# Hybrid attention layer in fp32 on TensorE: the rotary part of the softmax scores as two products of stacked rows instead of three

## The chip, the cores and the metric

The kernel runs on one core of one Trainium2 chip, in one launch. The metric is the device time of a run in microseconds (us); less is better. All data is fp32. Large matrix products are done in a "high and low" form: an operand x is split into xH, its value rounded to the matmul type fp32r, and xL = x - xH, again in fp32r. A product of two such operands is the sum of three matmuls (high times high, high times low, low times high) into one PSUM bank.

## The reference, cut to what matters

One decoder layer: an input projection that feeds two groups of heads (stick-breaking attention, 8 heads of 64; softmax attention with low-rank queries and keys, 4 heads), an output projection with a residual, and a SwiGLU feed-forward part. There are 1024 tokens and 1024 model columns. What matters here is the softmax group. Each of its heads has 128 plain columns (NOPE) and 64 rotary columns (ROPE); the rotary key is one for all four heads:

```python
def causal_softmax_attention(q, k, v):        # q, k: 192 columns a head, v: 128
    scale = MLA_QK_DIM ** -0.5
    for i in range(S // BLOCK_Q):
        s = einsum('bthd,bshd->bhts', q[:, q0:kend], k[:, :kend]) * scale
        p = softmax(where(causal, s, -inf), axis=-1)
        outs.append(einsum('bhts,bshd->bthd', p, v[:, :kend]))
...
q = concatenate([q[..., :128], apply_rope(q[..., 128:], positions)], axis=-1)
k_rope = broadcast_to(apply_rope(k_rope, positions), (B, S, 4, 64))
k = concatenate([k_nope, k_rope], axis=-1)
```

## The kernel before, in words

**Stages.** The program goes through input projections, an up-projection of queries and keys by token tiles of 128 (`up_tile`), the softmax heads, the stick-breaking heads, the output projection and the feed-forward part. The engines run one instruction list each and meet at semaphores. Tokens are held in reverse order, so the keys that a query tile may see are the columns from its own start to the end of the row.

**Softmax heads.** The four heads are worked in two pairs p, two heads e in each. A unit is one query tile of one head. `UNITS` lists 16 units for a pair: both heads go through the tiles in `ORDER0 = [7, 1, 5, 3, 2, 4, 0, 6]`, and tile i has 8 - i blocks of 128 keys, so a head's units have 1, 7, 3, 5, 6, 4, 8 and 2 blocks. This text numbers the units 0 to 31 through both pairs (unit 0 has 1 block, unit 1 has 7, unit 8 has 1 again) and writes S(u) for the scores, T(u) for the transposes and V(u) for the products with the values of unit u.

- S(u) on TensorE (`qk`, `mla_scores`, L1901 to L1907, through `three`, L1688): for each chunk of up to 512 keys, three matmuls of the plain columns (`mqH`, `mqL` with `mkH`, `mkL`), three of the rotary columns, all with 128 contraction rows, and in the first chunk one small bf16 matmul that adds the causal mask. There are 12 chunks in a head and 48 in all.
- `nmx` on VectorE (L1374) takes the row maximum from PSUM, ScalarE does the exponential into `pm` (L873), TensorE transposes `pm` block by block (L1933), ScalarE (L827) and VectorE (L1358) copy the result to `pmT`, and TensorE multiplies it with the values (L1944).
- The order on TensorE is S(u+2), T(u), V(u-1), then the next u. T(u) waits for the exponential of u and for the copy of T(u-1) by ScalarE. On ScalarE step u is: exponential of u, copy of T(u-2), then, in some steps, one extra instruction. On VectorE step u is: maximum of u, copy of T(u-2), the division for unit u-3 (`rden`, `o_mla`), then the extra instruction. So T(u) hangs on S(u+1) through maximum(u+1), exponential(u+1) and the copy of T(u-1).

**The rotary operands.** `QRK[:, p, :]` holds the rotary queries of a pair: 64 rows of head 0 above 64 rows of head 1. `mrH[p]`, `mrL[p]` are their high and low parts over all 128 rows. A head must not see the other head's rows, so there are two key operands for each part, `KRH[e]` and `KRL[e]`, that hold the rotary key in the 64 rows of head e and zeros in the other 64. GpSimd writes the zeros (`rope_key_zero`), ScalarE the high part (`rope_key_high`, L752), VectorE the low part (`rope_key_low`, L1308).

**The extra instructions.** Splits of operands for later heads are put into steps by hand: `SPLIT_AT` maps (pair, step) to what is split. Each costs one copy of 128 x 1024 on ScalarE (L747) and then one subtraction on VectorE (L1297) that waits for it. Before: steps 3 and 5 prepare head 1 of pair 0 (q and k), step 4 the second rotary key (`rope_key_high(1)`, `rope_key_low(1)`), steps 9, 10 and 12 the rotary queries, q and k of pair 1's head 0, steps 17 and 19 (written (1, 1) and (1, 3)) q and k of its head 1. `mla_ready` (L1970) makes TensorE wait for them by counts of `m_l`, `kr_zero` and `kr_l`. The splits of head 0 of pair 0 stand in `turn_out` and `first_split`, in two parts: tokens 128 to 1023 (EARLY) ahead of unit 0, tokens 0 to 127 (LATE) in step 2. Between S(1) and S(2) TensorE transposes the last token tile (`turn`).

**Transfers.** The SP queue issues nearly all transfers in program order, waits included. In the softmax stage it has nothing to do until `stack_head` (L437), which fills the operands of the first stick-breaking heads after unit 23. `stack_head` already puts the high rows of a head above its low rows in one operand and does the scores in two matmuls.

## Time and profile before

| | |
|---|---|
| median of 3 runs | 1360.83 us (1360.55 to 1362.74) |
| the profiled execution, its own time | 1363.38 us |
| its span, first to last instruction | 1361.6 us |
| TensorE matmul busy | 1301.8 us, 96% of the span |
| VectorE, ScalarE, GpSimd busy | 810.5, 554.9, 63.4 us |
| softmax stage, from S(0) to the first stick-breaking scores | 313.8 to 424.2 us of the span |

Times in rows are us from the span's start unless marked ns. A matmul's listed duration includes the part that overlaps the next one, so what a matmul costs in a stream is the distance from its start to the next start. In the chain of waits "<-" names what ended the idle time before an instruction.

### The profile page before, as it was taken

How to read it: one execution, taken by the hardware profiler on the slowest of the kernel's cores; microseconds unless marked ns; L12 is line 12 of the kernel's file. 1: busy time of each engine (PE TensorE's matmuls, PEld its weight loads, DVE VectorE, ACT ScalarE, POOL GpSimd, SP SyncE). 2: the span in 40 equal slices, each digit the busy share in tenths (PEclk: the TensorE clock that was granted, in tenths of full speed). 3: DMA queues.
4: the chain of work that ended last, by engine and by line, in shares of the span. 5: the costliest groups of instructions: out<-in, count | busy, mean ns of one | idle time of the engine just before them, and what ended most of it. 6: DMA issues, size and time to landing. Idle time of an engine off the chain costs nothing.

```text
span 1361.6 us, 17167 instructions
## 1 busy us (share of the span) xinstructions
PE 1301.8 (96%) x6708; PEld 1083.3 (80%) x6708; DVE 810.5 (60%) x1118; ACT 554.9 (41%) x890; POOL 63.4 (5%) x71
## 2 busy tenths in 40 slices
PE   3999999998999999899989999999999999999998
PEld 2678888896888888788867888888888888887886
DVE  7534567686556888953588665566655643334333
ACT  4512312585435778861275333333333322232221
POOL 1100200131000001000000000000000000001001
PEclk9999999999999999999999999999999999999999
DMA  9253445100011333401042212222122145447443
GB/s 382 72 231 124 168 188 188 49 1 1 2 39 40 78 79 77 171 16 62 32 185 93 93 63 78 93 93 89 56 89 93 62 145 183 154 145 262 140 145 126
DMA packets 38989, 149.25 MB, mean 110 GB/s; under 512 B 4352, under 2 KB 4480, under 8 KB 37376
## 3 DMA queue, kind: packets, MB, share of 16 engines
q1 hardware_dynamic: 36576, 139.80, 29.9%
q0 software_dynamic: 2336, 8.39, 1.7%
q8 instruction: 52, 0.85, 0.3%
q14 instruction: 25, 0.20, 0.0%
HBM read 117.77 MB, written 24.12 MB: 104 GB/s over the span
## 4 chain that ended last, share of the span: by engine, by line
PE 84%; DVE 8%; issue 3%; ACT 3%; DMA 1%; POOL 1%; SPq 0%; DVEq 0%; ACTq 0%
PE ps L2189 28%; PE ps L1701 13%; PE ps L1690 10%; PE ps L1692 10%; PE ps L1691 10%; DVE left L1408 3%; PE ps L1966 2%; PE ps L1944 2%; PE ps L1933 1%; PE ps L1953 1%; PE ps L1911 1%; DMA ada<-ada 1%; DVE beta L1413 1%; PE ps L1734 1%; ACT omb L907 1%
## 5 line engine op out<-in xcount | busy, mean ns | idle before, releaser
L1690 PE MATMUL ps<-TH,dWH 128*128 128x512 f32 x352 | 137.1, 390 | 0.9 <-DVE yst L1665 0.9
L1692 PE MATMUL ps<-TH,dWL 128*128 128x512 f32 x352 | 137.0, 389 | 0.0
L1691 PE MATMUL ps<-TL,dWH 128*128 128x512 f32 x352 | 136.9, 389 | 0.0
L2189 PE MATMUL ps<-h2H,slH 128*128 128x512 f32 x320 | 124.6, 389 | 0.0
L2189 PE MATMUL ps<-h2H,slL 128*128 128x512 f32 x320 | 124.5, 389 | 0.0
L2189 PE MATMUL ps<-h2L,slH 128*128 128x512 f32 x320 | 124.5, 389 | 0.0
L1624 DVE TENSOR_TENSOR TL<-traw,TH 128x512 fp32r<-128x512 f32 x44 | 30.5, 693 | 134.5 <-ACT TH L1029 134.5
L1009 ACT ACTIVATE slH<-ssum 128x512 fp32r<-128x512 f32 x80 | 50.4, 632 | 140.4 <-PE ps L2189 96.4
L1029 ACT ACTIVATE TH<-traw 128x512 fp32r<-128x512 f32 x44 | 27.8, 632 | 164.1 <-PE ps L1692 155.6
L1408 DVE TENSOR_TENSOR_SCAN left<-omb 128x255 f32<-128x255 f32 (+5 forms) x64 | 86.4, 1350 | 10.8 <-ACT omb L907 10.8
L1690 PEld LDWEIGHTS ps<-TH,dWH 128*128 128x128 f32 x352 | 66.1, 188 | 15.2 <-DVE yst L1665 1.3
L1692 PEld LDWEIGHTS ps<-TH,dWL 128*128 128x128 f32 x352 | 66.1, 188 | 13.8
L1691 PEld LDWEIGHTS ps<-TL,dWH 128*128 128x128 f32 x352 | 66.1, 188 | 13.7
L1966 PE MATMUL ps<-VS,wT 128*128 128x64 f32 x576 | 71.5, 269 | 0.3 <-DVE o_sb L1394 0.3
L2189 PEld LDWEIGHTS ps<-h2H,slH 128*128 128x128 f32 x320 | 60.1, 188 | 12.7 <-issue 0.3
L2189 PEld LDWEIGHTS ps<-h2L,slH 128*128 128x128 f32 x320 | 60.1, 188 | 12.5
L2189 PEld LDWEIGHTS ps<-h2H,slL 128*128 128x128 f32 x320 | 60.1, 188 | 12.4
L1966 PEld LDWEIGHTS ps<-VS,wT 128*128 128x128 f32 x576 | 69.4, 192 | 0.5 <-DVE o_sb L1394 0.5
L1602 DVE TENSOR_TENSOR slL<-ssum,slH 128x512 fp32r<-128x512 f32 x80 | 54.9, 688 | 18.2 <-ACT slH L1009 18.2
L1106 DVE TENSOR_TENSOR WL<-raw,WH 128x1024 fp32r<-128x1024 f32 x34 | 43.2, 1269 | 32.3 <-ACT WH L648 32.2
L1602 DVE TENSOR_TENSOR slL<-sraw,slH 128x512 fp32r<-128x512 f32 x60 | 41.2, 689 | 35.4 <-ACT slH L1009 35.4
L1626 DVE TENSOR_TENSOR dWL<-draw,dWH 128x1024 fp32r<-128x1024 f32 x44 | 53.9, 1225 | 11.0 <-ACT dWH L1031 11.0
(325 smaller groups left out, 3030.1 us busy)
## 6 DMA issues: line engine op xcount, KB each, us to landing
ada<-ada SPq DMA_DIRECT2D x12, 2048.0 KB, 9.1
draw<-down SPq DMA_DIRECT2D x44, 512.0 KB, 3.7
sraw<-gu SPq DMA_DIRECT2D x20, 1024.0 KB, 5.9
raw<-win SPq DMA_DIRECT2D x22, 512.0 KB, 4.5
traw<-t_spill_d SPq DMA_DIRECT2D x44, 256.0 KB, 3.9
t_spill_d<-tst SPq DMA_DIRECT2D x20, 512.0 KB, 3.0
x_in<-xT SPq DMA_DIRECT2D x4, 1024.0 KB, 8.6
qkl_spill_d<-qkl SPq DMA_DIRECT2D x8, 512.0 KB, 3.4
```

The lines of the kernel that those rows point to most:

```text
L1009: A(slH[q][:], operand(u, q), ACT.Copy).then_inc(sem["g_h"], 1)
L1106: V.tensor_tensor(WL[par % 2][:], raw[r % 2][:], WH[par % 2][:], ALU.subtract).then_inc(sem["split_l"], 1)
L1408: V.tensor_tensor_scan(left[v % 2][:, 1:n], omb[v % 2][:, 0:n - 1], omb[v % 2][:, 0:n - 1], 1.0, ALU.mult, ALU.bypass).then_inc(sem["s_sca ...
L1602: V.tensor_tensor(slL[q][:], operand(u, q), slH[q][:], ALU.subtract).then_inc(sem["g_l"], 1)
L1624: V.tensor_tensor(TL[d % 2][:], traw[d % 2][:], TH[d % 2][:], ALU.subtract).then_inc(sem["tl_done"], 1)
L1626: V.tensor_tensor(dWL[d % 2][:], draw[d % 2][:], dWH[d % 2][:], ALU.subtract).then_inc(sem["d_l"], 1)
L1690: mm(out, lh, rh, start=first, stop=False)
L1691: mm(out, lh, rl, start=False, stop=False)
L1692: return mm(out, ll, rh, start=False, stop=last)
L1701: last = mm(ps[:, b + hf, :], l[s][:, j * P:(j + 1) * P], cut(r, j, half(hf)), start=(j == 0 and k == 0), stop=(j == KD - 1 and k == 2))
L1966: last = mm(ps[:, bank, c:c + SBD], wT[v % 2][:, k * P:(k + 1) * P], VS[:, qt + k, (2 * i + e) * SBD:(2 * i + e + 1) * SBD], start=(k == 0 ...
L2189: last = mm(ps[:, Q_BANK[q], :], l[q][:, w], r[:, c, :], start=(c == 0 and k == 0 and q not in (Q_G2, Q_S4)), stop=(c == 3 and k == 2), sk ...
```

## The change

The high and the low rotary query rows of one head, 64 each, are stacked into one operand of 128 rows, `headR[p][e]`. `KRH` now holds the high rotary key in both halves, without zeros. One matmul of `headR` with `KRH` then gives (high + low) times high, and one of `headR` with `KRL[e]`, zeros beside the low rows as before, gives high times low.

- `mla_scores`: two rotary matmuls for each chunk instead of three. Units 0 and 1 (three chunks) keep three matmuls, with 64 contraction rows.
- The high part goes into its own 64 rows of `headR` by ScalarE, the low part into 64 rows of `mrL[p]` by VectorE. The low rows then have to move to the other 64 rows: new `rope_low` transfers within SBUF on the SP queue, ahead of `stack_head`. There are five: head 0 of pair 0 in two parts (64 x 896 and 64 x 128), the three other heads with 64 x 1024.
- The rotary queries are split by head. Step 4 gets ("r", 0, 1) in place of `rope_key_high(1)`, whose work is gone (`KRH` is written once, by one copy over 128 rows at the place of the first); `rope_key_low(1)` stays in step 4. Step 9 has ("r", 1, 0), now 64 rows. Step 14 gets ("r", 1, 1), which is new there.
- Two of the four zero fills of GpSimd are gone. `mla_ready` waits for the new counts and for the transfers. `headKH0` moves to another place in SBUF.

```diff
-SPLIT_AT = {(0, 3): ("q", 0, 1), (0, 5): ("k", 0, 1), (0, 9): ("r", 1, 0), (0, 10): ("q", 1, 0), (0, 12): ("k", 1, 0),
+SPLIT_AT = {(0, 3): ("q", 0, 1), (0, 4): ("r", 0, 1), (0, 5): ("k", 0, 1), (0, 9): ("r", 1, 0), (0, 10): ("q", 1, 0), (0, 12): ("k", 1, 0), (0, 14): ("r", 1, 1),
             (1, 1): ("q", 1, 1), (1, 3): ("k", 1, 1)}
...
-    KRH = [at("KRH0", [P, S], F32R, 102), at("KRH1", [P, S], F32R, 26)]
+    KRH = at("KRH", [P, S], F32R, 102)
...
-    mrH = [at("mrH0", [P, S], F32R, 138), at("mrH1", [P, S], F32R, 142)]
+    headR = [[at("headR00", [P, S], F32R, 138), at("headR01", [P, S], F32R, 26)], [at("headR10", [P, S], F32R, 142), at("headR11", [P, S], F32R, 146)]]
...
+        def rope_low(p, e, name, t=slice(0, S)):
+
+            own, other = slice(64 * e, 64 * e + 64), slice(64 - 64 * e, 128 - 64 * e)
+            sp.wait_ge(sem["m_l"], 4 if name == "late" else SPLIT_ORDER.index(("r", p, e)) + 1)
+            sp.dma_start(headR[p][e][other, t].bitcast(F32), mrL[p][own, t].bitcast(F32)).then_inc(rope_in[name][0], 16)
+
+        rope_low(0, 0, "early", EARLY)
+        rope_low(0, 0, "late", LATE)
+        for p, e in ((0, 1), (1, 0), (1, 1)):
+            rope_low(p, e, (p, e))
         for s, n in QKL.values():
             sp.wait_ge(qkl_out[s], 16 + 16 * n)
...
-            if m == 2:
-                pool.wait_ge(sem["kr_turn"], 1)
-                rope_key_zero(KRH, 0)
...
-            if p:
+            if p and (what, e) != ("r", 1):
                 act.wait_ge(sem["m_qk"], after(NU * (p - 1) + (7 if e == 0 else NU - 1)))
-            dst, src = {"r": (mrH[p], QRK[:, p, t]), ...}[what]
-            A(dst[:, t], src, ACT.Copy).then_inc(sem["m_h"], 1)
+            own = slice(64 * e, 64 * e + 64) if what == "r" else slice(0, P)
+            dst, src = {"r": (headR[p][e], QRK[:, p, :]), ...}[what]
+            A(dst[own, t], src[own, t], ACT.Copy).then_inc(sem["m_h"], 1)
...
-            if u == 4:
-                rope_key_high(1)
             if (p, v) in SPLIT_AT:
                 mla_split(*SPLIT_AT[p, v])
...
-            dve.wait_ge(sem["kr_h"], e + 1)
-            V.tensor_tensor(KRL[e][o, :], QRK[o, 2, :], KRH[e][o, :], ALU.subtract).then_inc(sem["kr_l"], 1)
+            dve.wait_ge(sem["kr_h"], 1)
+            V.tensor_tensor(KRL[e][o, :], QRK[o, 2, :], KRH[o, :], ALU.subtract).then_inc(sem["kr_l"], 1)
...
-            last = three(out, mrH[p][:, q], mrL[p][:, q], KRH[e][:, k], KRL[e][:, k], False, not diagonal)
+            if (p, e) == (0, 0) and q0 // P in ORDER0[:2]:
+                last = three(out, headR[0][0][0:64, q], mrL[0][0:64, q], KRH[0:64, k], KRL[0][0:64, k], False, not diagonal)
+            else:
+                mm(out, headR[p][e][:, q], KRH[:, k], start=False, stop=False)
+                last = mm(out, headR[p][e][:, q], KRL[e][:, k], start=False, stop=not diagonal)
...
                 pe.wait_ge(sem["m_l"], 3)
-                pe.wait_ge(sem["kr_zero"], 2)
                 pe.wait_ge(sem["kr_l"], 1)
+            elif u == 2:
+                pe.wait_ge(*rope_in["early"])
+                pe.wait_ge(sem["kr_zero"], 1)
             elif u == ORDER0.index(0):
                 pe.wait_ge(sem["m_l"], 6)
+                pe.wait_ge(*rope_in["late"])
             elif v == 0:
-                pe.wait_ge(sem["m_l"], 6 + 5 * p)
+                pe.wait_ge(sem["m_l"], SPLIT_ORDER.index(("k", p, 0)) + 1)
+                pe.wait_ge(*rope_in[p, 0])
...
```

## Rows read from the trace of the kernel before

**Rows 1.** Busy time by stretch, one for each softmax head; columns: stretch, length, five engines, clock, DMA.

```profile
313.80:342.35 28.55, 25.14 (x161) 21.34 (x161) 16.97 (x36) 14.06 (x31) 1.83 (x2) 0.94 0.00 1
342.35:370.40 28.05, 26.45 (x191) 23.27 (x190) 16.09 (x34) 12.11 (x27) 0.00 (x0) 1.00 0.00 1
370.40:397.67 27.27, 26.45 (x191) 23.34 (x190) 15.13 (x33) 11.16 (x26) 0.95 (x1) 1.00 0.04 8
397.67:424.18 26.51, 26.08 (x191) 23.21 (x190) 12.92 (x31) 9.27 (x24) 1.08 (x3) 1.00 0.22 51
```

**Rows 2.** Timeline, last rotary products of units 7 and 14; columns: start, duration, instruction.

```profile
338.06 0.28 PE L1692 MATMUL ps<-KRH,mrL 128*128 128x256 f32 x1
338.18 0.23 PE L1906 MATMUL ps<-mask_mla,identb 128*128 128x128 bf16 x1
...
365.31 0.39 PE L1692 MATMUL ps<-KRH,mrL 128*128 128x512 f32 x1
365.54 0.82 PE L1933 MATMUL ps<-ident,pm 128*128 128x128 f32 x6
```

**Rows 3.** Timeline of the first head, from maximum(2) to T(5) and V(4).

```profile
322.44 0.56 DVE L1374 TENSOR_REDUCE nmx<-ps 128x1 f32<-128x384 f32 x1 [1.59 <-PE ps L1906]
...
332.43 1.22 DVE L1308 TENSOR_TENSOR KRL<-QRK,KRH 64x1024 fp32r<-64x1024 f32 x1 [1.76 <-ACT KRH L752]
...
335.46 1.06 ACT L747 ACTIVATE mkH<-KN 128x1024 fp32r<-128x1024 f32 x1
...
336.55 1.23 DVE L1297 TENSOR_TENSOR mkL<-KN,mkH 128x1024 fp32r<-128x1024 f32 x1 [1.26 <-ACT mkH L747]
...
340.62 0.63 PE L1933 MATMUL ps<-ident,pm 128*128 128x128 f32 x4 [2.22 <-ACT pmT L827]
...
341.09 1.50 PE L1944 MATMUL ps<-VM,pmT 128*128 128x128 f32 x12
```

**Rows 4.** Timeline of the second head: maximum(9), and T(10) at the end of the chain.

```profile
347.66 1.09 DVE L1374 TENSOR_REDUCE nmx<-ps 128x1 f32<-128x896 f32 x1 [2.01 <-PE ps L1692]
...
358.04 0.30 PE L1933 MATMUL ps<-ident,pm 128*128 128x128 f32 x1 [0.94 <-ACT pmT L827]
```

**Rows 5.** Timeline from maximum(14) to T(14).

```profile
365.74 1.22 DVE L1374 TENSOR_REDUCE nmx<-ps 128x1 f32<-128x1024 f32 x1 [2.22 <-PE ps L1692]
...
368.10 0.48 ACT L827 ACTIVATE pmT<-ps 128x384 f32<-128x384 f32 x1
368.29 0.42 DVE L1374 TENSOR_REDUCE nmx<-ps 128x1 f32<-128x256 f32 x1 [0.23 <-PE ps L1906]
...
369.40 0.48 ACT L873 ACTIVATE pm<-ps,nmx 128x256 f32<-128x256 f32 x1 [0.82 <-PE ps L1933]
...
369.87 0.37 ACT L827 ACTIVATE pmT<-ps 128x256 f32<-128x256 f32 x1
...
371.17 0.39 PE L1933 MATMUL ps<-ident,pm 128*128 128x128 f32 x2
```

**Rows 6.** Timeline of the third head: maximum(17), and T(19) at the chain's end.

```profile
375.71 1.09 DVE L1374 TENSOR_REDUCE nmx<-ps 128x1 f32<-128x896 f32 x1 [2.02 <-PE ps L1692]
...
388.64 0.41 PE L1933 MATMUL ps<-ident,pm 128*128 128x128 f32 x2
```

**Rows 7.** Timeline of TensorE, where 32-column products stand between full ones.

```profile
49.73 0.61 PE L1769 MATMUL ps<-hH,WL 128*128 128x512 f32 x2
50.28 1.92 PE L1734 MATMUL ps<-ada,silu_w 128*32 128x512 f32 x16
52.13 0.50 PE L1690 MATMUL ps<-hH,WH 128*128 128x512 f32 x1
52.47 0.40 PE L1691 MATMUL ps<-hL,WH 128*128 128x512 f32 x1
```

**Rows 8.** The tile headQ, its transfers from issue to landing.

```profile
DMA to landing us min/median/max: 2.9/3.4/4.2
```

**Rows 9.** Timeline, the first matmul of S(0), and the idle time before it.

```profile
313.87 0.30 PE L1690 MATMUL ps<-mkH,mqH 128*128 128x128 f32 x1 [3.02 <-issue]
```

More of the change, by code:

```diff
@@ L237, in build @@
     headQ = [at("headQ0", [P, S], F32R, 98), at("headQ1", [P, S], F32R, 122)]
-    headKH = [at("headKH0", [P, S], F32R, 102), at("headKH1", [P, S], F32R, 126)]
+    headKH = [at("headKH0", [P, S], F32R, 106), at("headKH1", [P, S], F32R, 126)]
     headKL = [at("headKL0", [P, S], F32R, 138), at("headKL1", [P, S], F32R, 130)]
@@ L310, in build @@
     qkl_out = xin_in + ada1_in[:1]
+    rope_in = {"early": (ada1_in[1], 32), "late": (ada1_in[2], 32), (0, 1): (ada1_in[3], 32), (1, 0): (ada1_in[1], 48), (1, 1): (ada1_in[2], 48)}
     head_in = [ctx.enter_context(nc.semaphore(f"head_in{e}")) for e in range(2)]
@@ L582, in _ @@
             s = m % 2
-            if m in (3, 7):
-                pool.wait_ge(sem["kr_zero"], 1 if m == 3 else 2)
+            if m == 7:
+                pool.wait_ge(sem["kr_zero"], 1)
             pool.wait_ge(sem["q_ms"], m + 1)
@@ L588, in _ @@
             nc.gpsimd.tensor_tensor(rstd[:, s, 4:8], qms[:, s, 4:8], nhalf[:, 0:4], ALU.pow).then_inc(sem["rk_done"], 1)
-            if m in (2, 6):
+            if m == 6:
                 pool.wait_ge(sem["rk_done"], after(m))
-            if m == 2:
-                pool.wait_ge(sem["kr_turn"], 1)
-                rope_key_zero(KRH, 0)
-            if m == 6:
                 pool.wait_ge(sem["ll_done"], after(NT - 1))
@@ L599, in _ @@
         pool.wait_ge(sem["tr_done"], after(NT - 1))
-        rope_key_zero(KRH, 1)
         rope_key_zero(KRL, 1)
@@ L742, in mla_split, with rope_key_high @@
         def mla_split(what, p, e, t=slice(0, S)):
-            if p:
+            if p and (what, e) != ("r", 1):
                 act.wait_ge(sem["m_qk"], after(NU * (p - 1) + (7 if e == 0 else NU - 1)))
-            dst, src = {"r": (mrH[p], QRK[:, p, t]), "q": (mqH[e], QN[:, 2 * p + e, t]), "k": (mkH[e], KN[:, 2 * p + e, t])}[what]
-            A(dst[:, t], src, ACT.Copy).then_inc(sem["m_h"], 1)
-        def rope_key_high(e):
-            o = slice(64 * e, 64 * e + 64)
-            A(KRH[e][o, :], QRK[o, 2, :], ACT.Copy).then_inc(sem["kr_h"], 1)
+            own = slice(64 * e, 64 * e + 64) if what == "r" else slice(0, P)
+            dst, src = {"r": (headR[p][e], QRK[:, p, :]), "q": (mqH[e], QN[:, 2 * p + e, :]), "k": (mkH[e], KN[:, 2 * p + e, :])}[what]
+            A(dst[own, t], src[own, t], ACT.Copy).then_inc(sem["m_h"], 1)
+        def rope_key_high():
+            A(KRH[:], QRK[:, 2, :], ACT.Copy).then_inc(sem["kr_h"], 1)
         def turn_out(tt):
@@ L805, in up_tile @@
                 act.wait_ge(sem["kr_out"], 1)
-                rope_key_high(0)
+                rope_key_high()
         def one3(ap):
@@ L1295, in mla_split @@
             dve.wait_ge(sem["m_h"], k + 1)
-            lo, x, hi = {"r": (mrL[p], QRK[:, p, t], mrH[p]), "q": (mqL[e], QN[:, 2 * p + e, t], mqH[e]), "k": (mkL[e], KN[:, 2 * p + e, t], mkH[e])}[what]
-            V.tensor_tensor(lo[:, t], x, hi[:, t], ALU.subtract).then_inc(sem["m_l"], 1)
+            own = slice(64 * e, 64 * e + 64) if what == "r" else slice(0, P)
+            lo, x, hi = {"r": (mrL[p], QRK[:, p, :], headR[p][e]), "q": (mqL[e], QN[:, 2 * p + e, :], mqH[e]), "k": (mkL[e], KN[:, 2 * p + e, :], mkH[e])}[what]
+            V.tensor_tensor(lo[own, t], x[own, t], hi[own, t], ALU.subtract).then_inc(sem["m_l"], 1)
         def first_split(k, t):
@@ L1974, in mla_ready @@
                 pe.wait_ge(sem["m_l"], 3)
-                pe.wait_ge(sem["kr_zero"], 2)
                 pe.wait_ge(sem["kr_l"], 1)
+            elif u == 2:
+                pe.wait_ge(*rope_in["early"])
+                pe.wait_ge(sem["kr_zero"], 1)
             elif u == ORDER0.index(0):
                 pe.wait_ge(sem["m_l"], 6)
+                pe.wait_ge(*rope_in["late"])
             elif v == 0:
-                pe.wait_ge(sem["m_l"], 6 + 5 * p)
+                pe.wait_ge(sem["m_l"], SPLIT_ORDER.index(("k", p, 0)) + 1)
+                pe.wait_ge(*rope_in[p, 0])
             elif v == NU // 2:
-                pe.wait_ge(sem["m_l"], 8 + 5 * p)
+                pe.wait_ge(sem["m_l"], SPLIT_ORDER.index(("k", p, 1)) + 1)
+                pe.wait_ge(*rope_in[p, 1])
             if u == NU // 2:
-                pe.wait_ge(sem["kr_zero"], 4)
+                pe.wait_ge(sem["kr_zero"], 2)
                 pe.wait_ge(sem["kr_l"], 2)
```

## The prediction

> **What bounds the kernel now.** I read the page first: TensorE is busy nearly everywhere. Then the busy times by stretch, for the four softmax heads, since only there does the change touch TensorE's work [rows 1]. TensorE has the same 191 matmuls in the last three stretches (the first, where the stage fills, has 161), yet the four take 28.55, 28.05, 27.27 and 26.51 us. The last head has no split of operands in it, the first three have; so in the first three something besides TensorE sets the end for a part of the time. Then the timeline of each head, to see where TensorE stands idle before a T(u) and what let it go on. The reader is to see in it two kinds of stretch: those in which matmuls follow each other without a gap, where a removed matmul is time gained, and those in which ScalarE and VectorE hand work to each other without a pause while TensorE waits at the end, where a removed matmul only makes that wait longer.
>
> **The matmuls removed.** In a stream a 512-column product costs 0.23 us (365.31 to 365.54) and a 256-column one 0.12 (338.06 to 338.18) [rows 2]. The 384-column one I take between these, 0.18, and for 128 columns 0.11, a little under the 0.12 of the four transposes of that width from 340.62 to 341.09 [rows 3]. One product less in each chunk saves by unit size: 8 blocks 0.46, 7 blocks 0.41, 6 blocks 0.35, 5 blocks 0.34, 4 blocks 0.23, 3 blocks 0.18, 2 blocks 0.12, 1 block 0.11; together 2.20 a head and 8.80 for four. Units 0 and 1 keep their third product, 0.52: 8.28 us less TensorE work. That is the most that can be gained. How much of it arrives is a question for each stretch.
>
> **First head, units 2 to 7.** From maximum(2) at 322.44 to T(5) at 340.62 ScalarE and VectorE pass work to each other in one chain: maximum, exponential, copy, split, subtraction, next maximum, through the late splits of step 2 and the splits of steps 3, 4 and 5 [rows 3]. T(5) comes after 2.22 us of idle TensorE, released by ScalarE's copy. The chain starts at the end of S(2), so S(2)'s 0.18 is gained. What S(3) to S(7) save (0.34 + 0.35 + 0.23 + 0.46 + 0.12 = 1.50) lies inside the chain and is lost. Step 4 itself doesn't get longer, though it gets a second subtraction: now ScalarE copies the key for 1.06 us and VectorE stands idle for 1.76 us waiting for it, then subtracts for 1.22 [rows 3]. After the change ScalarE copies the queries in the same place, VectorE does the key's subtraction in its idle time, for which nothing has to be waited, and the new one starts at 332.4 as the old one did. If that idle time weren't there, the second subtraction would cost its 1.22.
>
> **Second head, units 8 to 15.** S(8) 0.11 and S(9) 0.41 are gained: T(6) to T(8) follow their predecessors without waiting. From the end of S(9) (maximum(9) at 347.66) to T(10) at 358.04, after 0.94 us idle, the splits of steps 9 and 10 make a chain again [rows 4], and S(10), S(11), S(12) are lost. The rotary split of step 9 is now 64 rows instead of 128; the 64-row subtraction took 1.22 and the 128-row one 1.23 [rows 3], so I count no gain. Then S(13) 0.23 and S(14) 0.46 are gained; the split of step 12 has over a microsecond of cover.
>
> **The new split in step 14** is the one part that adds to a chain. Before, maximum(15) follows at 368.29, soon after S(15), and T(14) at 371.17 waits for nobody [rows 5]. After, ScalarE's copy in step 14 ends at 368.58 (368.10 + 0.48); the split's copy ends 1.06 - 0.11 later (such instructions overlap by about 0.1), 369.53; the subtraction takes 1.23, to 370.78; maximum(15) 0.42, to 371.1; exponential(15) 0.48, to 371.65; the copy of T(13) 0.37, to 372.0; T(14) at 372.1. That is 6.36 us from maximum(14) instead of 5.43: a loss of 0.93, and what S(15) and S(16) save (0.23) is lost with it. It bites because step 15 is a unit of two blocks, with little work on TensorE around it to cover a split.
>
> **Third and fourth heads.** S(17) 0.41 is gained. From maximum(17) at 375.71 to T(19) at 388.64 the chain of the splits in steps 17 and 19 holds [rows 6]; S(18) to S(21) are lost. S(22) 0.46 is gained. T(21) waits for a copy that hangs on the maximum and exponential of the 8-block unit 22, as T(5) and T(13) do in their heads, so S(23) is lost. In the fourth head S(24) to S(30) are gained (0.11 + 0.41 + 0.18 + 0.34 + 0.35 + 0.23 + 0.46 = 2.08), S(31) is not, for the same reason.
>
> **Sum so far:** 0.18 + 0.52 + 0.69 + 0.41 + 0.46 + 2.08 = 4.34 gained, 0.93 lost: 3.41 us.
>
> **The 64-row products of units 0 and 1.** No row shows one. The nearest shows TensorE going over to products that use a part of the array, and back [rows 7]: two products before the change-over take 0.55 instead of 0.46 (49.73 to 50.28), the first after it 0.34 instead of 0.23; 0.2 for a round trip, more if the way out has a drain of its own. There are three such trips (three chunks), all before S(2), where TensorE is the path. I take 0.25 each, 0.75; the bounds are 0 and 2.4 (the round trips, and in addition nine weight loads of 0.19 that are no longer hidden, if such loads can't run ahead). The Trainium skill, in "TensorEngine Tiling (Array Packing)", Overview, Key Properties, says that changing the tiling mode drains TensorE. By that rule alone the price would be one pipeline drain for each of six changes, about the overlap of two neighbouring matmuls (0.39 - 0.23), so 1.0 as an estimate; it speaks against the change, by little.
>
> **Transfers.** Five of them, on an SP queue that has nothing else to do then; `stack_head` stands behind them, but needs unit 23, long after the last. A transfer within SBUF of this size landed 2.9 to 4.2 us after its issue [rows 8]. The tightest is (0, 1): its low part is ready at 332.43 + 1.22 = 333.65, landed by 337.9, and S(8) can't start before V(4) is over, 341.09 + 12 x 0.11, about 342.4 [rows 3]. 4.5 us of cover; cost nothing; if a transfer took 10 us, it would cost one or two. For "late", "early" and pair 1 the cover is longer. The two zero fills removed from GpSimd, and the copy of the key removed from step 4, were on no path.
>
> **Forecast.** 3.41 - 0.75 = 2.66 us less. The stage is followed by work that hangs on its end, so everything behind moves with it. The profiled execution took 1363.38 (a span of 1361.6, and 1.8 around it) and the median is 1360.83; the sum is a difference within the profiled one, and I take it off the median: 1358.2. About 0.2%, 2.7 us, is what a measurement of this kernel can tell from no change, and the forecast lies on that line.
>
> **Rivals.**
> 1. TensorE is the bound throughout, the chains yield as it gets faster: the whole 8.28 comes, 1352.6. For it: 96% busy. Against: the idle 2.22 and 0.94 us, released by ScalarE [rows 3, 4]. Chance 0.07.
> 2. Step 14's split finds cover that I don't see: then 0.93 + 0.23 more, 1357.0. Chance 0.12.
> 3. The 64-row products cost their upper bound: 3.41 - 2.4, 1359.8. Or the chains hold on for a unit longer here and there, for the same time. Chance 0.17.
> 4. **Slower: the clock.** Before S(0) TensorE was idle for 3.02 us [rows 9], and the first head's granted clock is 0.94 [rows 1]: 0.06 x 2 x 28.55 = 3.4 us at 1.2 instead of 2.4 GHz, which costs 1.7. The change makes TensorE's idle times longer wherever it is lost inside a chain: before T(5), T(10), T(14), T(17) and T(19). If the clock fell once, 1359.9; it is slower than before from the second fall on, and by more than 0.2% with four (4 x 1.7 - 2.66 = 4.1): 1364.9. The idle 2.22 us before T(5) didn't bring it down before, and becomes 2.34. The Trainium skill, in "TensorE: Matmul & The Clock Gate", Part 1, says that the throttled state is the default and activity releases it; that is the rule by which this rival would come true. Four falls 0.05, one to three 0.05.
> 5. The change doesn't do what it says, in that the rows arrive late and S(8), S(16) or S(24) waits: 1360 to 1362. Chance 0.02.
>
> The forecast itself has 0.52, from 1357.2 to 1359.2 by the roundings of the terms. Faster by over 0.2%: half of the forecast's share, rivals 1 and 2: 0.45. Slower: 0.06. The range reaches to rivals 2 and 3 and the single fall of the clock, with a half us of scatter of the median: 1356.2 to 1360.9.
>
> **What would show it.** In the profile after: 45 rotary matmuls fewer; TensorE idle before T(5) about 2.3 us with T(5) still 18.2 us after maximum(2); T(10) still 10.4 after maximum(9); T(14) 6.4 us after maximum(14) instead of 5.4, with idle TensorE before it; the four stretches between first scores, before 28.55, 28.05, 27.27 and 26.51, at 29.1 (0.75 for the 64-row products, less 0.18), 26.8 (less 1.21), 27.3 (0.93 more at T(14), less 0.87) and 24.4 us (less 2.08); no wait of TensorE on a transfer; the clock's one low stretch where it was. The forecast is wrong if T(5) or T(10) come closer to their maxima, if S(1) takes over 1 us longer, or if a second stretch at the low clock shows.

## The result, and the profile after

| | before | after |
|---|---|---|
| median, 20 runs each | 1363.67 us (1360.55 to 1366.19) | 1366.82 us (1363.03 to 1369.67) |
| the profiled execution, its own time | 1363.38 | 1368.87 |
| its span | 1361.6 | 1367.1 |
| softmax stage, S(0) to the first stick-breaking scores | 110.32 | 114.82 |
| stick-breaking scores, first to last | 153.78 | 154.48 |

The ratio is 1.0025, 95% interval 1.0016 to 1.0033: slower by 0.25%, 3.15 us by the medians, where 2.66 us less was forecast. The time lies outside the range. So would the forecast gain have done: the base of the forecast, 1360.83, was a median of three runs, the median of twenty is 1363.67, and 1363.67 - 2.66 is 1361.0, just above the range's 1360.9. Both kernels scatter by more than 5 us, and the scatter goes with TensorE's mean granted clock: executions of the kernel after at 0.994 took 1363 to 1364 us, at 0.989 they took 1368.6 to 1369.7; those of the kernel before had 0.994 to 0.998. The profiled execution of after is one with much low clock, so its 5.5 us are not the typical difference.

The page of the kernel after, its rows of busy time and, in 40 slices, TensorE's granted clock.

```profile
PE 1302.8 (95%) x6663; PEld 1081.2 (79%) x6663; DVE 812.8 (59%) x1120; ACT 556.0 (41%) x891; POOL 61.7 (5%) x69
...
PEclk9999999997999999999999999999999999999999
```

There are 45 matmuls fewer, as forecast, yet TensorE is busy 1.0 us longer. The clock row has a 7 in the tenth slice, where the first softmax head lies; before there was none. Busy times by stretch of the kernel after (columns as in [rows 1]): first the four heads, then the first two heads cut where the clock changes.

```profile
313.99:348.67 34.68, 30.26 (x152) 24.15 (x152) 18.26 (x37) 13.98 (x31) 0.94 (x1) 0.75 0.04 9
348.67:376.79 28.12, 25.54 (x178) 22.62 (x178) 15.93 (x33) 12.31 (x25) 0.00 (x0) 0.95 0.05 10
376.79:404.37 27.58, 24.43 (x180) 21.48 (x178) 16.21 (x36) 11.99 (x29) 0.95 (x1) 1.00 0.09 19
404.37:428.80 24.43, 23.88 (x179) 21.27 (x178) 12.93 (x31) 9.27 (x24) 1.08 (x3) 1.00 0.24 56
...
313.99:330.90 16.91, 15.95 (x52) 11.82 (x53) 6.27 (x16) 4.82 (x13) 0.94 (x1) 0.50 0.01 3
330.90:348.00 17.10, 13.64 (x98) 11.66 (x97) 12.00 (x22) 9.00 (x18) 0.00 (x0) 1.00 0.07 16
348.00:351.40 3.40, 3.40 (x20) 3.40 (x19) 0.81 (x3) 0.17 (x1) 0.00 (x0) 0.50 0.00 0
```

Against [rows 1] the first head takes 34.68 us instead of 28.55, the second 28.12 instead of 28.05, the third 27.58 instead of 27.27, the fourth 24.43 instead of 26.51. The last one gives what was forecast for it (24.4). The first loses all of it and more: TensorE ran at 1.2 GHz for 17.1 us on end (from 313.8), where the kernel before had 3.4 us, and again for 3.4 us from 348.0 on. Timeline of the kernel after (start, duration, instruction): one line of S(0) and two of S(1), then the maxima and transposes that answer to [rows 3 to 6] and [rows 9].

```profile
313.99 0.44 PE L1695 MATMUL ps<-mkH,mqH 128*128 128x128 f32 x1 [3.01 <-issue]
...
317.82 0.62 PE L1696 MATMUL ps<-KRL,headR 64*128 64x512 f32 x1
318.25 0.62 PE L1697 MATMUL ps<-KRH,mrL 64*128 64x512 f32 x1
...
326.84 0.56 DVE L1379 TENSOR_REDUCE nmx<-ps 128x1 f32<-128x384 f32 x1 [2.31 <-PE ps L1915]
...
346.61 0.63 PE L1942 MATMUL ps<-ident,pm 128*128 128x128 f32 x4 [2.33 <-ACT pmT L833]
...
354.74 1.09 DVE L1379 TENSOR_REDUCE nmx<-ps 128x1 f32<-128x896 f32 x1 [1.60 <-PE ps L1913]
...
365.11 0.52 PE L1942 MATMUL ps<-ident,pm 128*128 128x128 f32 x3 [1.28 <-ACT pmT L833]
...
372.13 1.22 DVE L1379 TENSOR_REDUCE nmx<-ps 128x1 f32<-128x1024 f32 x1 [1.55 <-PE ps L1913]
...
376.08 1.22 DVE L1302 TENSOR_TENSOR mrL<-QRK,headR 64x1024 fp32r<-64x1024 f32 x1 [1.63 <-ACT headR L754]
377.34 0.42 DVE L1379 TENSOR_REDUCE nmx<-ps 128x1 f32<-128x256 f32 x1
...
378.73 1.06 PE L1942 MATMUL ps<-ident,pm 128*128 128x128 f32 x8 [1.12 <-ACT pmT L833]
```

The idle time before S(0) is the same 3.0 us. The clock gave 0.43 us for a product of 512 columns (317.82 to 318.25) instead of the 0.23 of [rows 2]. Most of the chains stand where the forecast put them: T(5) after 2.33 us of idle TensorE, T(10) 10.37 us after maximum(9), T(14) 6.60 us after maximum(14). But T(5) comes 19.77 us after maximum(2) (326.84 to 346.61) instead of the forecast 18.2, since the first part of that chain lies in the low stretch. And two of the forecast's own signs of being wrong are there: S(1) takes 5.7 us (315.67 to 321.35) instead of 4.2 (314.60 to 318.81 before), and there is a second stretch at the low clock.

### The profile page after: what moved, and what is told of

Same layout as the page of the kernel before. It is cut to its first block, busy times and chain, and to the rows that moved or that the text cites. A ratio compares the mean times of both kernels' runs of the same rounds, so it can differ in the third digit from the quotient of the medians.

```text
span 1367.1 us, 17081 instructions
## 1 busy us (share of the span) xinstructions
PE 1302.8 (95%) x6663; PEld 1081.2 (79%) x6663; DVE 812.8 (59%) x1120; ACT 556.0 (41%) x891; POOL 61.7 (5%) x69
## 4 chain that ended last, share of the span: by engine, by line
PE 82%; DVE 8%; issue 4%; ACT 3%; DMA 1%; POOL 1%; SPq 0%; DVEq 0%; ACTq 0%
PE ps L2203 28%; PE ps L1706 13%; PE ps L1695 10%; PE ps L1697 10%; PE ps L1696 10%; DVE left L1413 3%; PE ps L1975 2%; PE ps L1953 2%; PE ps L1962 1%; PE ps L1942 1%; PE ps L1920 1%; PE ps L1739 1%; DVE nmx L1379 1%; DVE beta L1418 1%; DMA ada<-ada 1%
## 5 line engine op out<-in xcount | busy, mean ns | idle before, releaser
L1696 PEld LDWEIGHTS ps<-TL,dWH 128*128 128x128 f32 x352 | 66.1, 188 | 13.7
L1607 DVE TENSOR_TENSOR slL<-ssum,slH 128x512 fp32r<-128x512 f32 x80 | 54.9, 688 | 18.2 <-ACT slH L1013 18.2
```

The costliest lines, as they stand in the source:

```text
L1607: V.tensor_tensor(slL[q][:], operand(u, q), slH[q][:], ALU.subtract).then_inc(sem["g_l"], 1)
L1696: mm(out, lh, rl, start=False, stop=False)
```

## The experiments

The quoted expectations call it Theory A that the 64-row products of units 0 and 1 are the cause; its weak form is that they keep a low clock from rising, its strong form that they bring down a high one. Each ratio is to runs of the kernel before on the same chips.

| kernel | median (range, runs) | ratio to before, 95% | softmax stage |
|---|---|---|---|
| b_rows64 | 1369.28 (1367.45 to 1369.75, 5) | 1.0037 (1.0024 to 1.0051) | 116.90 |
| a_rows128 | 1361.57 (1358.29 to 1363.42, 11) | 0.9984 (0.9973 to 0.9995) | 108.35 |
| b_warm | 1360.91 (1360.32 to 1363.61, 11) | 0.9983 (0.9974 to 0.9992) | 110.41 |
| a_warm | 1361.94 (1359.38 to 1363.88, 11) | 0.9988 (0.9979 to 0.9997) | 106.51 |
| a_step16 | 1364.90 (1361.66 to 1368.15, 11) | 1.0011 (0.9999 to 1.0023) | 112.46 |
| b_warm_fill | 1361.35 (1358.95 to 1363.18, 12) | 0.9985 (0.9976 to 0.9994) | 108.78 |
| a_warm_fill | 1359.75 (1358.09 to 1361.22, 11) | 0.9974 (0.9965 to 0.9983) | 106.51 |
| a_all | 1356.90 (1356.51 to 1359.34, 5) | 0.9961 (0.9946 to 0.9975) | 104.63 |
| b_all64 | 1377.80 (1373.70 to 1378.70, 4) | 1.0095 (1.0075 to 1.0116) | 126.48 |
| a_all_dve | 1357.59 (1355.58 to 1359.17, 6) | 0.9957 (0.9942 to 0.9972) | 104.61 |

The names begin with a for edits of the kernel after, b for edits of the kernel before. The stage lengths and all rows are from the one profiled execution of each; what was low or high in the other runs only their mean granted clock tells.

### The 64-row products alone, and taken away: b_rows64, a_rows128

b_rows64 is the kernel before with one edit. The other 64 rows met zeros, so nothing is left out.

```diff
+            if (p, e) == (0, 0) and q0 // P in ORDER0[:2]:
+                last = three(out, mrH[0][0:64, q], mrL[0][0:64, q], KRH[0][0:64, k], KRL[0][0:64, k], False, not diagonal)
+            else:
                 last = three(out, mrH[p][:, q], mrL[p][:, q], KRH[e][:, k], KRL[e][:, k], False, not diagonal)
```

> The kernel before, with only the rotary products of units 0 and 1 cut to 64 contraction rows (upper half of the same operands), as the changed kernel has them; nothing else. Theory A (the 64-row products keep the clock low after the idle time before S(0)): the low stretch that starts at about 314 us lasts some 17 us instead of 3.4, S(2) to V(1) take twice as long, and the run is 4 to 6 us slower than before. Theory B (the clock stays low because of the idle times that the shorter S(u) leave, the 64-row products only cost their change-overs): low stretch of 3.4 us, run 0.5 to 1.5 us slower.

a_rows128 is the kernel after; units 0 and 1 get back 128-row operands, a zero fill and two more copies on ScalarE.

```diff
+    KRZ = [at("KRZ", [P, S], F32R, 82)]
+    mr0 = at("mr0", [P, S], F32R, 86)
...
-                last = three(out, headR[0][0][0:64, q], mrL[0][0:64, q], KRH[0:64, k], KRL[0][0:64, k], False, not diagonal)
+                last = three(out, mr0[:, q], mrL[0][:, q], KRZ[0][:, k], KRL[0][:, k], False, not diagonal)
```

> The changed kernel, but units 0 and 1 do their three rotary products with 128 rows, from a copy of the high rows of both heads and a key with zeros beside it, as before the change. Theory A: one low stretch of 3.4 us at S(0), perhaps one more after T(5); 3 us faster than the kernel before (the 3.4 us of the forecast without the 64-row term), 6 to 7 faster than the changed kernel. Theory B: the long low stretch stays, within 1 us of the changed kernel.

First head of b_rows64, busy times; its stretch at the low clock; T(5) from its timeline:

```profile
313.33:347.82 34.49, 31.16 (x161) 25.07 (x161) 17.00 (x36) 14.01 (x31) 1.83 (x2) 0.77 0.00 1
...
314.88:328.53 13.65, 12.69 (x40) 8.97 (x39) 4.25 (x11) 3.75 (x12) 1.83 (x2) 0.50 0.01 1
...
345.03 0.63 PE L1936 MATMUL ps<-ident,pm 128*128 128x128 f32 x4 [2.22 <-ACT pmT L827]
```

The same of a_rows128, whose clock was low from 312.4 on, ahead of S(0):

```profile
313.32:342.79 29.47, 24.72 (x152) 20.97 (x152) 18.08 (x37) 14.83 (x34) 0.94 (x1) 0.90 0.05 11
...
313.32:319.19 5.87, 5.87 (x19) 4.96 (x20) 2.67 (x9) 2.37 (x6) 0.00 (x0) 0.50 0.01 3
...
341.07 0.63 PE L1953 MATMUL ps<-ident,pm 128*128 128x128 f32 x4 [2.33 <-ACT pmT L840]
```

The low stretch doesn't begin at the same place in every execution, so like has to be compared with like:

| profiled execution | products of S(0), S(1) | clock fell | low for | S(0) to T(5) |
|---|---|---|---|---|
| before | 128 rows | 315.1, 1.2 us behind the start of S(0) | 3.41 us | 26.75 us |
| b_rows64 | 64 rows | 314.9, 1.55 us behind the start of S(0) | 13.65 us | 31.70 us |
| a_rows128 | 128 rows | 312.4, ahead of S(0) | 6.83 us | 27.75 us |
| after | 64 rows | 313.8, ahead of S(0) | 17.07 us | 32.62 us |

In either pair the 64-row products keep the clock low for 10.2 us longer, and T(5) comes 4.95 and 4.87 us later. It is nine products on half the rows and, in b_rows64, nothing else. The first head of b_rows64 is longer by more, 5.9 us (34.49 against 28.55 in [rows 1]), because it also has 2.2 us of another low stretch, behind T(5). The runs without a trace agree: b_rows64 has mean granted clocks of 0.991 to 0.993 and the kernel before 0.994 to 0.998, the kernel after 0.989 to 0.994 and a_rows128 0.994 to 0.998. By the ratios b_rows64 is 0.37% slower than before, and a_rows128 0.16% faster, where the kernel after was 0.25% slower. That settles where most of the time went. By size the expectations were met in part: the stretch of b_rows64 was to be some 17 us long, that of a_rows128 3.4, and a_rows128 was to be 3 us faster than before, not 2.2. The 3.4 us of low clock from 348.0 on, after T(5), are another matter: b_rows64 had them too (at 345.6), a_rows128 not.

### A warm TensorE ahead of S(0): b_warm, a_warm

The kernel has 44 small bf16 products ahead of S(0), which end 3.0 us before it [rows 9]. More of them fill the time up to S(0).

```diff
-WARM_MLA = 44
+WARM_MLA = 96
```

> The kernel before, with 96 instead of 44 of the small bf16 products ahead of S(0), so that TensorE isn't idle while the first splits run; S(0) starts when it did. Both theories: no low stretch at S(0), 1.5 to 2 us faster than before, and less scatter between runs, if that scatter is the clock's.

> The changed kernel with the same 96 small products ahead of S(0). Theory A in its strong form (64-row products count too little, whatever stood before): the clock still falls in S(1) or behind it. Theory A in its weak form (they only fail to raise a clock that is already low) and theory B: no low stretch at S(0); then 4 to 5 us faster than the kernel before, 2 to 3 faster than the kernel before with the same products, by the sum of the forecast, which held no clock. S(0) and S(1) at the full clock also give the price of the 64-row products: forecast 0.75 us, bounds 0 to 2.4.

First head of a_warm, then, in its timeline, the second chunk's rotary products of S(1) between full products:

```profile
313.63:341.24 27.61, 22.85 (x152) 18.59 (x152) 18.08 (x37) 14.00 (x31) 0.94 (x1) 1.00 0.05 11
```

```profile
314.92 0.39 PE L1696 MATMUL ps<-mkL,mqH 128*128 128x512 f32 x1
315.15 0.40 PE L1697 MATMUL ps<-mkH,mqL 128*128 128x512 f32 x1
315.48 0.50 PE L1695 MATMUL ps<-KRH,headR 64*128 64x512 f32 x1
315.81 0.39 PE L1696 MATMUL ps<-KRL,headR 64*128 64x512 f32 x1
316.04 0.39 PE L1697 MATMUL ps<-KRH,mrL 64*128 64x512 f32 x1
316.37 0.23 PE L1915 MATMUL ps<-mask_mla,identb 128*128 128x128 bf16 x1
```

With the clock high at S(0), the same 64-row products leave it high in this execution: 1.00 in the first head. This is the weak form of Theory A. Here the price of a change-over can be read without the clock: a full stream has a pitch of 0.23 (314.92 to 315.15), so has the stream of 64-row products (315.81 to 316.04), while the way in takes 0.33 for each of two products (315.15 to 315.48 to 315.81) and the way out 0.33: 0.29 us a trip. By the ratios the warm products are worth 0.37% to the kernel after (1.0025 to 0.9988, 5.0 us) and 0.17% (2.3 us, where 1.5 to 2 was expected) to the kernel before.

a_warm still missed its expectation. It was to be 4 to 5 us faster than before and is 1.6 us faster (0.9988); it was to be 2 to 3 us faster than b_warm, and its median, 1361.94, is 1.0 us above b_warm's 1360.91. Its runs have mean granted clocks of 0.995 to 0.998, those of b_warm 0.996 to 1.000. So the profiled execution of a_warm, at 0.998, is one of its better ones, and warm products ahead of S(0) alone don't lay the change's gain bare.

The Trainium skill, in "TensorE: Matmul & The Clock Gate", Part 1, says that the throttled state is the default and activity releases it. That agrees with a high clock behind warm products; but TensorE was busy 15.95 of 16.91 us in the kernel after, and stayed at the low clock. Work of this kind did not release it here for that long, and the measurement decides.

b_warm shows the other low stretch by itself. Its busy times, cut where the clock changes, and T(5) from its timeline:

```profile
314.15:340.50 26.35, 23.02 (x154) 19.56 (x155) 16.90 (x36) 13.57 (x30) 1.83 (x2) 1.00 0.00 1
340.50:343.90 3.40, 3.40 (x19) 3.40 (x18) 0.80 (x3) 0.43 (x3) 0.00 (x0) 0.50 0.00 0
```

```profile
339.37 0.63 PE L1933 MATMUL ps<-ident,pm 128*128 128x128 f32 x4 [2.21 <-ACT pmT L827]
```

The 2.21 us of idle TensorE before T(5), the same as in [rows 3], was followed by a fall of the clock 1.1 us after T(5) in this execution; in the profiled ones of before, of a_warm (2.34 us) and of a_rows128 (2.33 us) there was none. In b_dve1 (below), the kernel before with one more VectorE instruction, it fell there too, after 2.21 us. And there the 3.01 us of idle time before S(0) brought no fall at all. So both waits are followed by a fall in some executions and not in others, in the kernel before already.

### The split of step 14 elsewhere: a_step16

```diff
-SPLIT_AT = {(0, 3): ("q", 0, 1), (0, 4): ("r", 0, 1), (0, 5): ("k", 0, 1), (0, 9): ("r", 1, 0), (0, 10): ("q", 1, 0), (0, 12): ("k", 1, 0), (0, 14): ("r", 1, 1),
-             (1, 1): ("q", 1, 1), (1, 3): ("k", 1, 1)}
+SPLIT_AT = {(0, 3): ("q", 0, 1), (0, 4): ("r", 0, 1), (0, 5): ("k", 0, 1), (0, 9): ("r", 1, 0), (0, 10): ("q", 1, 0), (0, 12): ("k", 1, 0),
+             (1, 0): ("r", 1, 1), (1, 1): ("q", 1, 1), (1, 3): ("k", 1, 1)}
```

> The changed kernel with its new split, (r, 1, 1), in step 16 instead of step 14. By the ledger of the forecast: T(14) follows maximum(14) by 5.2 us instead of 6.6, without idle time before it, and step 16, a one-block unit between large ones, hides the split: 1.2 us faster than the changed kernel, if the clock behaves alike in both. If the split costs the same wherever it stands: no difference, and idle time before T(16) or more before T(17).

Second and third head of a_step16:

```profile
346.65:374.78 28.13, 25.55 (x178) 22.62 (x178) 16.07 (x34) 12.09 (x27) 0.00 (x0) 0.95 0.05 10
374.78:401.38 26.60, 24.37 (x180) 21.54 (x178) 16.27 (x34) 12.21 (x27) 0.95 (x1) 1.00 0.09 20
```

T(14) no longer waits, and the stretch from S(16) on takes 26.60 us instead of 27.58. (S(16) stands ahead of T(14) in TensorE's order, so this loss falls into the third stretch.) The 1.0 us is most of the loss that was forecast at 0.93 and came to 1.17. The median's ratio, 1.0011, has 1 within its interval; the profile decides here, not the time. This kernel has the 64-row products too, and its clock was low for 13.65 us at S(0), from 315.2 on, and for 3.4 us behind T(5).

### The ledger at full clock: b_warm_fill, a_warm_fill

Warm products up to S(0) in both kernels, and 34 more in the idle time before T(5), into a PSUM bank that is free then.

```diff
-WARM_MLA = 44
+WARM_MLA = 88
...
+            if n == 5:
+                for _ in range(34):
+                    mm(ps[:, 3, 0:P], identb[:], identb[:], start=True, stop=True)
```

> The kernel before with the same two fills. About 1359 to 1360 us, scatter under 2 us; it gives the change without the clock: the changed kernel with fills is 2.7 us faster than this one if the ledger of the forecast holds, level with it if the ledger was wrong and the clock hid that.

> The changed kernel with 88 small products ahead of S(0) and 34 more ahead of T(5), where TensorE is idle for 2.5 us: no low stretch at S(0) nor behind T(5), in nearly every run. Theory (the whole miss is the clock): what is left is the ledger of the forecast, 2.7 us less than the kernel before with the same two fills, and the scatter between runs shrinks to under 2 us.

The four heads of b_warm_fill:

```profile
314.16:341.09 26.93, 25.49 (x195) 22.01 (x195) 16.91 (x36) 14.00 (x31) 1.83 (x2) 1.00 0.00 1
341.09:369.16 28.07, 26.45 (x192) 23.28 (x190) 16.09 (x34) 12.11 (x27) 0.00 (x0) 1.00 0.01 1
369.16:396.43 27.27, 26.45 (x192) 23.34 (x190) 15.14 (x33) 11.16 (x26) 0.95 (x1) 1.00 0.04 8
396.43:422.94 26.51, 26.08 (x192) 23.22 (x190) 12.92 (x31) 9.27 (x24) 1.08 (x3) 1.00 0.21 52
```

The four heads of a_warm_fill:

```profile
314.04:341.65 27.61, 24.75 (x186) 20.45 (x186) 18.08 (x37) 13.99 (x31) 0.94 (x1) 1.00 0.05 11
341.65:368.50 26.85, 24.27 (x180) 21.34 (x178) 15.94 (x33) 12.31 (x25) 0.00 (x0) 1.00 0.05 11
368.50:396.09 27.59, 24.43 (x179) 21.47 (x178) 16.21 (x36) 12.00 (x29) 0.95 (x1) 1.00 0.09 19
396.09:420.55 24.46, 23.91 (x179) 21.27 (x178) 12.92 (x31) 9.27 (x24) 1.08 (x3) 1.00 0.24 56
```

With every clock at 1.00 the differences are the ledger's: 0.68 more, 1.22 less, 0.32 more, 2.05 less, together 2.27 us less, where 2.66 was forecast. So the change is worth 2.27 us in the softmax stage as long as the clock holds. The medians, 1361.35 and 1359.75, differ by 1.60: the kernel after loses 0.70 us again behind the stage, which a later section takes up, and 2.27 - 0.70 is 1.57.

The scatter didn't shrink to under 2 us, as was expected. It is 4.2 us in b_warm_fill, whose median is also above the 1359 to 1360 expected, and 3.1 us in a_warm_fill. There is one more low stretch, near the start of the program. Busy times from 25 to 45 us, of a_warm_fill and, for comparison, of a_all (next section):

```profile
25.00:45.00 20.00, 15.99 (x84) 7.01 (x76) 13.72 (x18) 9.25 (x8) 0.13 (x1) 0.83 0.70 291
...
25.00:45.00 20.00, 15.37 (x94) 8.28 (x87) 16.54 (x21) 9.27 (x8) 0.09 (x1) 1.00 0.69 290
```

A clock of 0.83 over 20 us is 6.8 us at 1.2 GHz. b_warm_fill and after have the same 0.83 there, before has 0.91 (3.4 us), a_all and b_dve1 have 1.00. With 1.00 S(0) started at 311.2 and 311.3 us, with 0.83 at 314.0 to 314.2. The change does nothing in this part of the program; these nearly 3 us come and go from run to run and lie under every median here.

### All of it together: a_all

a_rows128, a_step16 and the two fills of the last section in one kernel.

> All together: the changed kernel, 128-row products in units 0 and 1, the new split in step 16, and both fills. 2.7 + 0.75 + 1.2 = 4.6 us faster than the kernel before with the fills, about 7 faster than the kernel before. Less than that if the extra copies for the 128-row products delay S(0).

0.9961 times before (0.9946 to 0.9975), faster than both kernels. The softmax stage takes 104.63 us, 5.7 less than before, and 4.15 less than the kernel before with the same fills, where 4.6 was expected; against the kernel before it is 5.3 us by the ratio, where about 7 was expected.

### 64 rows everywhere: b_all64

```diff
-            last = three(out, mrH[p][:, q], mrL[p][:, q], KRH[e][:, k], KRL[e][:, k], False, not diagonal)
+            o = slice(64 * e, 64 * e + 64)
+            last = three(out, mrH[p][o, q], mrL[p][o, q], KRH[e][o, k], KRL[e][o, k], False, not diagonal)
```

> The kernel before with all rotary products of all 32 units on the own 64 rows, three a chunk (the other rows meet zeros, so the result is the same). Prices so far: 0.29 us for a trip to 64 rows and back at the high clock, and in units 0 and 1, where the clock is low after the idle time, 6.6 us in all. Theory A (64-row products keep a low clock from rising but don't bring a high one down): 45 further chunks x 0.29 = 13.1 us, less what the waits of TensorE before T(5), T(10), T(13) and T(14) take up (about 3): 10 to 13, and with units 0 and 1 the softmax stage goes from 110.3 to between 126 and 130 us, ratio to before 1.011 to 1.015, one long low stretch at S(0) and none within the later streams. Rival B (they do bring a high clock down): low stretches in the later units too, the softmax stage over 140 us, ratio over 1.02.

Its first head cut where the clock changes, and the second and the fourth (the third also takes 29.63 us at a clock of 1.00):

```profile
313.07:335.90 22.83, 21.87 (x66) 15.10 (x66) 7.97 (x20) 7.14 (x17) 1.83 (x2) 0.50 0.00 1
335.90:350.65 14.75, 14.56 (x96) 11.22 (x95) 9.42 (x17) 6.84 (x14) 0.00 (x0) 1.00 0.00 1
...
350.65:380.28 29.63, 29.63 (x191) 22.80 (x190) 16.07 (x34) 12.11 (x27) 0.00 (x0) 1.00 0.00 1
...
409.91:439.55 29.64, 29.64 (x192) 22.80 (x190) 12.94 (x31) 9.27 (x24) 1.08 (x3) 1.00 0.19 46
```

The low stretch got longer still (23.9 us, from 312.1, ahead of S(0)), and once the clock was up, the 36 chunks of the three other heads, all with 64-row products, did not bring it down: that speaks against the strong form, in one execution. The fourth head, which had next to no waits, is 3.13 us longer than in [rows 1] for its 12 chunks, 0.26 a trip. All heads take the same 29.63 us: with this much work TensorE alone sets the pace and the chains of ScalarE and VectorE disappear in it. The stage met its expectation; the ratio, 1.0095, is a little below the expected 1.011 to 1.015.

### The 0.70 us behind the softmax stage: b_dve2, b_dve1, a_all_dve

Every variant of the kernel after so far took 154.4 to 154.5 us for the stick-breaking scores, every one of the kernel before 153.8, though the change touches nothing of VectorE's work there. VectorE's timeline shows two holes, at the stage's units 19 and 49; the first, in the kernel after:

```profile
476.36 2.28 DVE L1413 TENSOR_TENSOR_SCAN left<-omb 128x1023 f32<-128x1023 f32 x1
479.10 1.23 DVE L1418 TENSOR_TENSOR beta<-beta,left 128x1024 f32<-128x1024 f32 x1 [0.46 <-DVE left L1413]
```

Elsewhere the product follows 0.10 us after the scan. The change puts two subtractions more on VectorE, all long over by then. So VectorE's list was lengthened by instructions that nobody needs.

```diff
             if u == 4:
                 rope_key_low(1)
+            if u in (4, 15):
+                V.reciprocal(scr[:, u % 2:u % 2 + 1], nhalf[:, 0:1])
```

> The kernel before with two reciprocals of a single column more on VectorE, in steps 4 and 15, that nobody waits for; it then issues as many VectorE instructions ahead of the stick-breaking stage as the kernel after. Open is where the 0.70 us come from that every variant of the kernel after loses in the stick-breaking stage (154.48 us instead of 153.78), in two holes of 0.35 us between the scan and the product with beta, at the stage's units 19 and 49. Theory P, the place of an instruction in VectorE's list decides: the same two holes at units 19 and 49, stage 154.4 to 154.5 us. Rival Q, something in what the change does (the layout of SBUF, the transfers): no holes there, stage 153.7 to 153.8 us. The softmax stage stays within 0.3 us of 110.3 by both, where the clock falls as before.

> The same with one reciprocal more, in step 4. Theory P: the hole falls on another instruction; with two more it lies between the scan and the product, with none more it is nowhere to be seen, so with one more either of the two; if it is seen, it is at other instructions than units 19 and 49's products, and the stage is 153.8 to 154.5 us. Rival Q: as before, 153.7 to 153.8 us, no holes but the one at unit 58.

The same place in b_dve2:

```profile
470.89 2.28 DVE L1411 TENSOR_TENSOR_SCAN left<-omb 128x1023 f32<-128x1023 f32 x1
473.62 1.22 DVE L1416 TENSOR_TENSOR beta<-beta,left 128x1024 f32<-128x1024 f32 x1 [0.46 <-DVE left L1411]
```

And in b_dve1:

```profile
469.31 2.28 DVE L1411 TENSOR_TENSOR_SCAN left<-omb 128x1023 f32<-128x1023 f32 x1
471.69 1.23 DVE L1416 TENSOR_TENSOR beta<-beta,left 128x1024 f32<-128x1024 f32 x1
```

(These two kernels had one run each, 1363.14 and 1360.91 us; the profile is what was wanted.) Two instructions more in the kernel before make the same two holes, and the stick-breaking scores take 154.47 us; one more makes none, 153.76. Theory P holds: it is the place in VectorE's list that decides. All seven profiled kernels with two instructions more than before (after and its five variants so far, b_dve2) have the two holes at units 19 and 49, the four other variants of the kernel before with its own number have none. The last kernel takes the holes out of a_all with a third instruction:

> The kernel of a_all (units 0 and 1 with three 128-row rotary products, the split of step 14 in step 16, warm products ahead of S(0) and T(5)) with one reciprocal of a single column more on VectorE, in step 4, so that VectorE's list is three instructions longer than in the kernel before instead of two. If the place in the list decides and the stall moves to the instruction one earlier, it lies ahead of the scan, where VectorE waits for ScalarE for part of it anyway: the two holes between scan and product go, the stick-breaking stage is 153.8 to 154.2 us instead of 154.48, the softmax stage stays at 104.6 to 104.8, the median is 0.3 to 0.7 us under a_all's share of before: ratio 0.9955 to 0.996. If it only costs the same in another place: 154.4 to 154.5 us, ratio as a_all's 0.996.

153.77 us and neither of the two holes. The ratio, 0.9957, lies where it was expected, but the median, 1357.59, can't be told from a_all's 1356.90; the gain stands in the profile alone. (This profiled execution had the early low stretch, S(0) at 314.00 us, and that of a_all had not, 311.18.)

## Why the prediction was wrong

**The step that failed** is the price of the 64-row products, "I take 0.25 each, 0.75; the bounds are 0 and 2.4". It looked at a change-over between two neighbouring products, at the high clock, and at nothing else. The change-over was right (0.29). But these nine products stand in the one place of the stage where the clock is low or about to fall, behind 3.0 us of idle TensorE, and there they keep it low: by themselves, in b_rows64, they put off T(5) by 4.95 us, and 0.9 of that are the change-overs, instead of 0.75 forecast and 2.4 at most. The prediction had both facts in separate sections, the low stretch as something that stays "where it was", the products as work of known length, and never put them together.

**Rival 4** named the clock, and the wrong end of it. It expected falls of fixed length, each with a price of 1.7 us, in the waits that the change makes longer, and asked for more than one of them to be slower. What came was mostly one low stretch that would not end: 17.1 us instead of 3.4. Its own mechanism came too, once, at T(5), in the place it gave; without the 64-row products (a_rows128) the kernel was faster than before all the same. "The idle 2.22 us before T(5) didn't bring it down before" was read from one execution; b_warm and b_dve1 show a fall after 2.21.

**How much is the clock.** The kernel after spent 20.3 us of its stage at 1.2 GHz (16.91 + 3.40) and took 114.82 us, a_warm_fill none and 106.51: 8.3 us. For the kernel before it is 3.4 us at 1.2 GHz and 110.32 - 108.78 = 1.5 us. So in the profiled executions the clock turned a gain of 2.27 us into a loss of 4.50. In medians it turned 1.60 less (the two fill kernels) into 3.15 more: 4.75 us.

**The whole miss,** 8.6 us from 1358.2 to 1366.82, as an estimate from these numbers: 4.75 the clock, 0.7 behind the stage (below), 0.4 the ledger (2.66 - 2.27), and 2.8 the base. The prediction took its gain off the median of three runs, 1360.83, and gave that median half a microsecond of scatter; the twenty runs go from 1360.55 to 1366.19, with a median of 1363.67.

**Right, by the step:**
- Units 8 to 13 and 24 to 31: forecast 1.21 and 2.08 less, at full clock 1.22 and 2.05.
- The chains: T(10) 10.37 us after maximum(9) in the kernel after (forecast 10.4); T(5), at full clock, 339.92 - 321.75 = 18.17 us after maximum(2) in a_warm_fill (18.2), and 2.33 us of idle before it in the kernel after (about 2.3). What S(3) to S(7), S(10) to S(12) and S(18) to S(21) save is lost, as said.
- Against rival 1: of 8.28 us less TensorE work 2.27 arrived, at full clock too.
- The transfers cost nothing. From the kernel after, its five transfers into `headR`:

```profile
L450 SPq DMA_DIRECT2D headR<-mrL x5: 461/462/539, 311.4 to 377.3; - x5
DMA to landing us min/median/max: 1.7/2.8/2.8
```

They landed in 1.7 to 2.8 us; the 4.5 us of cover were ample, and nothing of TensorE waited for them.

**Right, but mis-sized:**
- The 64-row products at full clock: 0.87 us instead of 0.75 (S(0) to T(5) is 25.88 us in a_warm and 25.01 in a_all, which has 128-row products there).
- Step 14: 1.17 instead of 0.93. T(14) comes 6.60 us after maximum(14), not 6.36, where it was 5.43 before. The subtraction started 3.95 us after the maximum (372.13 to 376.08), where 3.79 was worked out, and maximum(15) 1.26 behind its start (376.08 to 377.34), where 1.15 was. (The prediction's sum has slips of its own, of a few hundredths: 371.1 + 0.48 is 371.58, not 371.65.) a_step16 shows that rival 2 was open to whoever looked for another step.
- The other terms sum to what was forecast: -2.66 + 0.12 + 0.24 is -2.30, against -2.27 measured.

**Missed altogether:** 0.70 us on VectorE behind the stage. "The stage is followed by work that hangs on its end, so everything behind moves with it" is true of what the instructions wait for, and not of how VectorE gets them.

**What stays open.** Why the clock rises after 3.4 or 6.8 us behind full products and not behind 64-row ones isn't shown; nor is why it stays low for some 9 us beyond S(1) (in the kernel after, from 321.35 to 330.9), with full rows again and one wait of 1.0 us. Why the idle time before S(0) or T(5) brings it down in one execution and not in the next was not tried. Nor is it shown whether the long low stretch makes the fall behind T(5) likelier: the three profiled kernels that had the one (after, b_rows64, a_step16) had the other, b_all64 had no idle time before T(5), and b_warm and b_dve1 fell there without it.

## What to carry to other kernels

Read the clock together with the place where new work lands: a matmul on part of the array's rows costs its change-over where the clock is high, and here some 4.9 us for nine of them where the clock is low and has to rise. Full-row operands with zeros are the cheaper way at such a place, and small products up to the first real one left the clock high there in all six profiled kernels that had them. Judge a change of this size by stage lengths at equal clock as well as by the median, since here the scatter of the clock was larger than the effect.
